# Out-projection of a hybrid decoder step: the order of VectorE's and ScalarE's work over its last six jobs

## The chip, the cores and the metric

One core of a Trainium2 chip runs the whole program. The metric is the device time of one execution in microseconds (us); lower is better. TensorE (PE) multiplies, VectorE (DVE), ScalarE (ACT) and GpSimd (POOL) work elementwise, SyncE (SP) issues the DMAs. Each engine takes its instructions strictly in the order in which they are written for it; they meet only through semaphores.

## The reference

One layer of a causal decoder over 1024 prompt tokens and 32 tokens of eight decoding sequences, width 1024, all in float32. The part that matters here:

```
mix = concat(attention(xn), short_conv(xn))      # xn = rms_norm(x)
h   = x + mix @ w_out                            # out-projection, 1024 x 1024
hn  = rms_norm(h, norm_ffn_g)                    # the second norm
y   = h + (silu(hn @ w_gate) * (hn @ w_up)) @ w_down     # FFN, hidden width 2816
out = rms_norm(y, norm_final_g)
```

with `rms_norm(x, g) = x * rsqrt(mean(x*x) + 1e-6) * g` over the 1024 channels. The program also returns the new keys, values and convolution states.

## The kernel before

Activations lie transposed: channels on the 128 partitions in KT = 8 tiles, 1056 tokens along the free axis in NC = 3 chunks of CH = 352 columns. A float32 product is made of three passes over operands split into a high and a low part (`act_hi`, `act_lo` for activations, `w_hi`, `w_lo` for weights). A *job* is one output tile n of one chunk c: 8 tiles x 3 passes = 24 matmuls of 352 columns into one of the PSUM banks 0 to 5.

The out-projection has 24 jobs in the order OUT_ORDER: c outer and n = 0, 1 inner (jobs 0 to 5), then n = 2, 3, 4 over all chunks (6 to 14), then for each chunk n = 5, 6, 7. So chunk 0 is complete with job 17, chunk 1 with job 20, chunk 2 with job 23. For every job

- VectorE adds the bank to the residual (`add_product`, line 1441; it counts `h_done`),
- ScalarE squares the new residual tile into one of six slots (`square`, line 1005; `h_sq`),
- VectorE adds the square to the chunk's running sum `ssum` (`add_squares`, lines 1448 and 1451; `h_ss`). In the kernel before this is called for job j - 1 behind the product of job j.

When a chunk's sum is complete, TensorE sums it over the partitions with a matrix of ones (`sum_of_squares`, line 805, into bank 6 or 7). Sum 0 stands behind job 18, sum 1 behind job 22 (SUMS_BEHIND = [18, 22]), and sum 2 behind the first job of the FFN:

```
pe.wait_ge(h_ss, chunk_end(c))      # 18, 21 and 24 additions
...
if i == 0:
    sum_of_squares(2)
```

Then `mean_square` (VectorE, line 1131), `take_root` (ScalarE, a Sqrt, line 886) and the reciprocal (VectorE, line 1137) give the chunk's factor. The normalised tile k of the chunk is made by `normal` (VectorE, line 1138, into one of two slots of `out32`), copied to `act_hi` by ScalarE (`normal_hi`, line 881), and its rest is put into `act_lo` by VectorE (`low`, line 1146). Eight such tiles make `norm(1, c)`. Slot i is free when the low part of i - 2 is done.

In the kernel before VectorE does the whole norm of chunk 0 behind product 18; products 19 to 22 with their additions, the mean of chunk 1, product 23 and the last two additions follow; then come norm 1, the mean of chunk 2 and norm 2. ScalarE follows the same order.

The first group of the FFN has 12 jobs, chunk outer and n inner (`FIRST_JOBS`: two gate tiles n = 0, 1 and two up tiles n = 2, 3). The first job of a chunk waits for all eight low parts of that chunk (`lo_done`). The up tiles n = 2, 3 reuse the banks of the gate tiles and wait for ScalarE's Silu of these (line 1011, `first_silu`, called one by one with `next(first_silus)`; those not yet taken are taken in `gates(0, 0, first=True)`). ScalarE loads a table when it changes between Sqrt and Silu.

GpSimd splits each weight unit of 128 x 1024 that the DMAs bring into `w_hi` (a cast, line 393) and `w_lo` (a subtraction, line 395), with a small gate instruction (line 391) ahead of them that waits until the unit three places before has been used. The first three units of the FFN follow the ends of jobs 21, 22 and 23, the fourth has a place of its own and follows directly. SyncE loads a unit as soon as the split of the unit two places before is done. POOL's and SP's orders are not touched by the diff.

Of the kernel before, what the change touches and what calls it, by code (L numbers as in the profile page):

```python
# [30 lines left out]
KT = D // P  # L31
# [4 lines left out]
NC = 3  # L36
# [33 lines left out]
def f32(ap):  # L70
    return ap.bitcast(F32)


def build(nc, xT, w, gains, taps, conv_state, state_k, state_v, yT, kT, v_out, conv_tail):
    with ExitStack() as ctx:
# [147 lines left out]
        def norm_slot(i):  # L223

            return out32[:, 2 + i % 2, :]

        def cols(c):
            return slice(CH * c, CH * (c + 1))
# [650 lines left out]
        def _(act):  # L879
            def copy(out, in_):  # L880
                return act.activation(out, in_, ACT.Copy)  # L881

            def take_root(which, c):
                act.wait_ge(mean_sq, NC * which + c + 1)
                r = rstd if which else r_in
                act.activation(r[:, cols(c)], r[:, cols(c)], ACT.Sqrt).then_inc(root, 1)

            def normal_hi(c, ks=range(KT)):
                for k in ks:
                    i = KT * c + k  # L890
                    act.wait_ge(y_done, i + 1)
                    copy(act_hi[:, k, cols(c)], norm_slot(i)).then_inc(hi_done, 1)
# [21 lines left out]
            for j in range(QK_JOBS, QK_JOBS + V_JOBS):  # L914
# [4 lines left out]
                i = j - QK_JOBS  # L919
# [80 lines left out]
            def square(which, j):  # L1000
                n, c = H_ORDERS[which][j]
                act.wait_ge(h_done, NC * KT * which + j + 1)
                if j >= 6:
                    act.wait_ge((h_ss, last_ss)[which], j - 5)
                act.activation(sq6[j % 6], res[:, n, cols(c)], ACT.Square).then_inc(h_sq, 1)

            def first_silu():

                for i, (f, c) in enumerate(FIRST_GATES):
                    act.wait_ge(job_done, OUT_JOB0 + 24 + FIRST_JOBS.index((f, c)) + 1)  # L1010
                    yield act.activation(silu[:, f, cols(c)], ps[:, 3 * f + c, 0:CH], ACT.Silu).then_inc(silu_done, 1)

            first_silus = first_silu()
            for j in range(NC * KT):
                square(0, j)
                if j in SUMS_BEHIND:
                    take_root(1, SUMS_BEHIND.index(j))
                if j == SUMS_BEHIND[0]:
                    normal_hi(0)
            next(first_silus)  # L1020
            normal_hi(1, range(0, 2))
            next(first_silus)
            normal_hi(1, range(2, 8))
            take_root(1, 2)
            normal_hi(2, range(0, 3))
            next(first_silus)
            normal_hi(2, range(3, 6))
            next(first_silus)
            normal_hi(2, range(6, 8))

            def gates(it, g, first=False):
                job = 72 * it + FFN_JOB0 + 36 * g
# [40 lines left out]
        def _(dve):  # L1073
# [50 lines left out]
            def mean_square(which, c):  # L1124

                if which == 0:
                    dve.wait_ge(ss_done, c + 1)
                else:
                    dve.wait_ge(ss_all, NC * (which - 1) + c + 1)
                bank = (c % 2, 6 + c % 2, c)[which]  # L1130
                dve.tensor_scalar((rstd if which else r_in)[:, cols(c)], ps[:, bank, 0:CH], 1.0 / D, EPS, ALU.mult, ALU.add).then_inc(mean_sq, 1)

            def normal(which, c, k, dst):

                if k == 0:
                    dve.wait_ge(root, NC * which + c + 1)
                    chain(dve.reciprocal(rstd[:, cols(c)], rstd[:, cols(c)]))  # L1137
                dve.scalar_tensor_tensor(dst, res[:, k, cols(c)], g_sb[:, which, k:k + 1], rstd[:, cols(c)],  # L1138
                                         ALU.mult, ALU.mult).then_inc(y_done, 1)

            def norm(which, c):

                def low(i):
                    k = i % KT
                    dve.wait_ge(hi_done, i + 1)
                    dve.tensor_tensor(act_lo[:, k, cols(c)], norm_slot(i), f32(act_hi[:, k, cols(c)]),  # L1146
                                      ALU.subtract).then_inc(lo_done, 1)

                for k in range(KT):
                    i = KT * c + k  # L1150
                    if i >= 2:
                        dve.wait_ge(lo_done, i - 1)
                    normal(which, c, k, norm_slot(i))
                    if k >= 1:
                        low(i - 1)
                low(KT * c + KT - 1)

            def raw_low(k):

# [274 lines left out]
            def add_product(which, j):  # L1434

                n, c = H_ORDERS[which][j]
                dve.wait_ge(job_done, (OUT_JOB0, LAST_JOB0)[which] + j + 1)
                if which == 0:
                    dve.wait_ge(x2_in[n], 16)
                bank = j % 6 if which == 0 else last_bank(j)  # L1440
                dve.tensor_tensor(res[:, n, cols(c)], ps[:, bank, 0:CH], res[:, n, cols(c)],  # L1441
                                  ALU.add).then_inc(h_done, 1)

            def add_squares(j):
                n, c = OUT_ORDER[j]
                dve.wait_ge(h_sq, j + 1)
                if n == 0:
                    dve.tensor_copy(ssum[:, cols(c)], sq6[j % 6]).then_inc(h_ss, 1)
                else:
                    dve.wait_ge(h_ss, OUT_ORDER.index((n - 1, c)) + 1)  # L1450
                    dve.tensor_tensor(ssum[:, cols(c)], ssum[:, cols(c)], sq6[j % 6], ALU.add).then_inc(h_ss, 1)

            for j in range(NC * KT):
                add_product(0, j)
                if j >= 1:
                    add_squares(j - 1)
                if j in SUMS_BEHIND:
                    mean_square(1, SUMS_BEHIND.index(j))
                if j == SUMS_BEHIND[0]:
                    norm(1, 0)  # L1460
            add_squares(NC * KT - 1)
            norm(1, 1)
            mean_square(1, 2)
            norm(1, 2)

            def hidden_of(it, g, first=False):
                for i in range(6):
# [8 lines left out]
            with dve.Fori(0, 5) as it:  # L1476
                for g in (1, 2):
                    hidden_of(it, g)
                    for i in range(NC * KT):
                        n, c = divmod(i, NC)  # L1480
# [83 lines left out]
SUMS_BEHIND = [18, 22]  # L1564
# [6 lines left out]
def last_bank(i):  # L1571

    return 3 + i % LAST_RING
# [165 lines left out]
```

## Time and profile before

| what | us |
|---|---|
| median of 3 runs | 1337.97 |
| lowest, highest | 1336.29, 1338.19 |
| the profiled execution, its own time | 1337.92 |
| its span, first to last instruction | 1336.1 |
| TensorE busy in the span | 1303.4 |
| VectorE busy | 474.6 |
| ScalarE busy | 238.3 |
| GpSimd busy | 504.9 |

The profiled execution took 1.8 us more than its span, and stands 0.05 under the median. TensorE is busy nearly throughout, so the table alone says little of any other engine: what they do matters only where TensorE waits for them. All times in the rows below are us from the start of the span.

### The profile page before, as it was taken

What the parts mean: (1) busy time and instruction counts of PE and PEld (TensorE: products, weight loads), DVE (VectorE), ACT (ScalarE), POOL (GpSimd) and SP (SyncE); (2) the same over time, 40 slices, a digit from 0 to 9 for tenths busy, and PEclk for the clock granted to TensorE, in tenths of its full rate; (3) what the DMA queues carried; (4) which work ended last, traced back from release to release, by engine and by line L of the source; (5) the groups of instructions that cost most, each with busy time, mean ns of one, the idle gap of its engine ahead of it and who ended that gap; (6) DMA issues with size and microseconds to landing.
All of it is one profiled execution on the core that took longest, in us unless ns stands there. A gap on an engine that the chain in (4) does not pass through costs nothing.

```text
span 1336.1 us, 20793 instructions
## 1 busy us (share of the span) xinstructions
PE 1303.4 (98%) x8488; PEld 1224.6 (92%) x8488; DVE 474.6 (36%) x884; ACT 238.3 (18%) x505; POOL 504.9 (38%) x476
## 2 busy tenths in 40 slices
PE   6999999999899999899999999999999999999996
PEld 6999987989565699899999999999999999999996
DVE  5854222344565432860212222221213130303056
ACT  6000110000666511331000010101010101010114
POOL 3443143222464332406434343434333333444435
PEclk9999999999999999999999999999999999999998
DMA  5534566252111131101111111111111111110103
GB/s 194 186 136 179 183 222 236 69 199 79 48 64 64 35 128 48 47 18 64 48 48 48 48 48 48 48 46 37 45 48 48 48 48 48 46 50 32 63 1 132
DMA packets 37940, 107.84 MB, mean 81 GB/s; under 512 B 4000, under 2 KB 16352, under 8 KB 36064
## 3 DMA queue, kind: packets, MB, share of 16 engines
q1 hardware_dynamic: 37856, 106.60, 22.4%
q8 instruction: 67, 1.10, 0.3%
q14 instruction: 17, 0.14, 0.0%
HBM read 95.73 MB, written 10.85 MB: 80 GB/s over the span
## 4 chain that ended last, share of the span: by engine, by line
PE 68%; DVE 4%; issue 1%; ACT 1%; DVEq 0%; ACTq 0%
PE ps L507 14%; PE ps L508 14%; PE ps L509 14%; PE ps L858 6%; PE ps L860 6%; PE ps L859 6%; PE ps L649 2%; PE ps L692 2%; PE ps L673 2%; DVE out L1138 1%; PE ps L667 1%; DVE work L1137 1%; DVE resid L1500 0%; DVE resid L1343 0%; DVE act_lo L1146 0%
## 5 line engine op out<-in xcount | busy, mean ns | idle before, releaser
L507 PE MATMUL ps<-act_hi,w_hi 128*128 128x352 f32 x1608 | 522.8, 325 | 10.5 <-DVE act_lo L1161 10.2
L508 PE MATMUL ps<-act_lo,w_hi 128*128 128x352 f32 x1608 | 516.5, 321 | 0.0
L509 PE MATMUL ps<-act_hi,w_lo 128*128 128x352 f32 x1608 | 516.3, 321 | 0.0
L507 PEld LDWEIGHTS ps<-act_hi,w_hi 128*128 128x128 f32 x1608 | 302.6, 188 | 24.6 <-issue 23.7
L508 PEld LDWEIGHTS ps<-act_lo,w_hi 128*128 128x128 f32 x1608 | 303.1, 188 | 0.2
L509 PEld LDWEIGHTS ps<-act_hi,w_lo 128*128 128x128 f32 x1608 | 302.3, 188 | 0.0
L391 POOL TENSOR_TENSOR gate_cell<-ones 128x1 f32<-128x1 f32 x92 | 18.1, 197 | 676.7 <-PE ps L509 462.0
L395 POOL TENSOR_TENSOR w_lo<-w_stage,w_hi 128x1024 fp32r<-128x1024 f32 x95 | 233.3, 2456 | 7.6
L1472 DVE TENSOR_TENSOR work<-ps,work 128x352 f32<-128x352 f32 x66 | 34.4, 524 | 443.4 <-PE ps L509 443.4
L858 PE MATMUL ps<-pair_hi,w_hi 128*128 128x352 f32 x504 | 162.7, 323 | 0.0
L1482 DVE TENSOR_TENSOR resid<-ps,resid 128x352 f32<-128x352 f32 x240 | 126.0, 525 | 102.7 <-PE ps L860 102.7
L859 PE MATMUL ps<-pair_lo,w_hi 128*128 128x352 f32 x504 | 162.2, 322 | 0.0
L860 PE MATMUL ps<-pair_hi,w_lo 128*128 128x352 f32 x504 | 162.1, 322 | 0.0
L393 POOL CAST w_hi<-w_stage 128x1024 fp32r<-128x1024 f32 x95 | 99.2, 1044 | 19.5 <-DVE work L1169 9.5
L1040 ACT ACTIVATE work<-ps 128x352 f32<-128x352 f32 x60 | 27.9, 465 | 401.3 <-PE ps L509 401.3
L860 PEld LDWEIGHTS ps<-pair_hi,w_lo 128*128 128x128 f32 x504 | 94.8, 188 | 0.0
L859 PEld LDWEIGHTS ps<-pair_lo,w_hi 128*128 128x128 f32 x504 | 94.7, 188 | 0.0
L858 PEld LDWEIGHTS ps<-pair_hi,w_hi 128*128 128x128 f32 x504 | 94.7, 188 | 0.0
L881 ACT ACTIVATE pair_hi<-work 128x352 fp32r<-128x352 f32 (+1 forms) x70 | 36.9, 531 | 289.5 <-DVE work L1472 211.1
L440 POOL TENSOR_SCALAR q_blk<-ident,row_rec 128x128 f32<-128x128 f32 x64 | 43.1, 685 | 78.3 <-DVE row_rec L1352 78.3
L471 POOL TENSOR_TENSOR pair_lo<-work,pair_hi 128x352 fp32r<-128x352 f32 x66 | 60.6, 948 | 0.0
L1441 DVE TENSOR_TENSOR resid<-ps,resid 128x352 f32<-128x352 f32 x48 | 25.0, 522 | 56.5 <-PE ps L509 47.9
(216 smaller groups left out, 1316.0 us busy)
## 6 DMA issues: line engine op xcount, KB each, us to landing
w_stage<-in_w SPq DMA_DIRECT2D x98, 512.0 KB, 3.5
resid<-in_state_k SPq DMA_DIRECT2D x8, 1792.0 KB, 8.0
v_buf<-in_state_v SPq DMA_DIRECT2D x14, 1024.0 KB, 5.2
resid<-in_xT SPq DMA_DIRECT2D x16, 528.0 KB, 7.5
out_yT<-resid SPq DMA_DIRECT2D x24, 176.0 KB, 1.8
q_d<-out SPq DMA_DIRECT2D x12, 176.0 KB, 4.3
out_kT<-out SPq DMA_DIRECT2D x12, 176.0 KB, 1.8
out_v<-out SPq DMA_DIRECT2D x16, 128.0 KB, 1.9
```

The lines of the kernel that those rows point to most:

```text
L393: pool.tensor_copy(hi, w_stage[:, stage, :]).then_inc(w_split, 1)
L395: pool.tensor_tensor(lo, w_stage[:, stage, :], f32(hi), ALU.subtract).then_inc(w_split, 1)
L440: pool.tensor_scalar(recip[t % 4][h], ident[:, :], row_rec[:, x:x + 1], None, ALU.mult).then_inc(spread, 1)
L471: pool.tensor_tensor(pair_lo[:, 2 * (g % 2) + f, cols(c)], silu[:, f, cols(c)], f32(pair_hi[:, 2 * (g % 2) + f, cols(c)]), ALU.subtract).t ...
L507: pe.matmul(out, hi, rhs_hi, start=first, stop=False)
L508: pe.matmul(out, hi, rhs_lo, start=False, stop=False)
L509: return pe.matmul(out, lo, rhs_hi, start=False, stop=last)
L858: pe.matmul(out, hi, x_hi, start=(f == 0), stop=False)
L859: pe.matmul(out, hi, x_lo, start=False, stop=False)
L860: mm = pe.matmul(out, lo, x_hi, start=False, stop=(f == 1))
L881: return act.activation(out, in_, ACT.Copy)
L1482: dve.tensor_tensor(res[:, n, cols(c)], ps[:, 6 + i % 2, 0:CH], res[:, n, cols(c)], ALU.add).then_inc(added, 1)
```

## The change

Only the order of calls in VectorE's and ScalarE's programs changes, from job 0 of the out-projection to the norm of chunk 2. Squares are added directly behind the product of the same job. The products and additions of jobs 19 to 23 are put between the tiles of the norms of chunks 0 and 1: 19 and 20 inside norm 0, 21 and 22 between the norms, 23 inside norm 1, that is behind chunk 1's reciprocal and its first two normals. `norm` becomes `normals`, which takes a range of tiles. ScalarE squares in the same places; it takes all Silus but the first two behind norm 2, where before two more stood inside it.

```diff
@@ ScalarE @@
             first_silus = first_silu()
-            for j in range(NC * KT):
+            for j in range(SUMS_BEHIND[0] + 1):
                 square(0, j)
-                if j in SUMS_BEHIND:
-                    take_root(1, SUMS_BEHIND.index(j))
-                if j == SUMS_BEHIND[0]:
-                    normal_hi(0)
+            take_root(1, 0)
+            normal_hi(0, range(0, 2))
+            square(0, 19)
+            normal_hi(0, range(2, 5))
+            square(0, 20)
+            normal_hi(0, range(5, 8))
+            square(0, 21)
+            square(0, 22)
+            take_root(1, 1)
+            normal_hi(1, range(0, 2))
+            square(0, 23)
+            normal_hi(1, range(2, 5))
             next(first_silus)
-            normal_hi(1, range(0, 2))
+            normal_hi(1, range(5, 8))
             next(first_silus)
-            normal_hi(1, range(2, 8))
             take_root(1, 2)
-            normal_hi(2, range(0, 3))
-            next(first_silus)
-            normal_hi(2, range(3, 6))
-            next(first_silus)
-            normal_hi(2, range(6, 8))
+            normal_hi(2, range(0, 8))
@@ VectorE @@
-            def norm(which, c):
+            def normals(which, c, ks):
...
-                for k in range(KT):
+                for k in ks:
                     i = KT * c + k
                     if i >= 2:
                         dve.wait_ge(lo_done, i - 1)
                     normal(which, c, k, norm_slot(i))
                     if k >= 1:
                         low(i - 1)
-                low(KT * c + KT - 1)
+                    if k == KT - 1:
+                        low(i)
...
-            for j in range(NC * KT):
+            for j in range(SUMS_BEHIND[0] + 1):
                 add_product(0, j)
-                if j >= 1:
-                    add_squares(j - 1)
-                if j in SUMS_BEHIND:
-                    mean_square(1, SUMS_BEHIND.index(j))
-                if j == SUMS_BEHIND[0]:
-                    norm(1, 0)
-            add_squares(NC * KT - 1)
-            norm(1, 1)
+                add_squares(j)
+            mean_square(1, 0)
+            normals(1, 0, range(0, 2))
+            add_product(0, 19)
+            normals(1, 0, range(2, 3))
+            add_squares(19)
+            normals(1, 0, range(3, 5))
+            add_product(0, 20)
+            normals(1, 0, range(5, 6))
+            add_squares(20)
+            normals(1, 0, range(6, 8))
+            add_product(0, 21)
+            add_squares(21)
+            add_product(0, 22)
+            mean_square(1, 1)
+            add_squares(22)
+            normals(1, 1, range(0, 2))
+            add_product(0, 23)
+            normals(1, 1, range(2, 3))
+            add_squares(23)
+            normals(1, 1, range(3, 8))
             mean_square(1, 2)
-            norm(1, 2)
+            normals(1, 2, range(0, 8))
```

## Rows read from the trace of the kernel before

**Rows 1.** The page, busy us, share of the span and instructions of each engine.
```profile
PE 1303.4 (98%) x8488; PEld 1224.6 (92%) x8488; DVE 474.6 (36%) x884; ACT 238.3 (18%) x505; POOL 504.9 (38%) x476
```

**Rows 2.** Waits of TensorE from 530 to 600: in total, times, longest.
```profile
PE ps L805 <- DVE work L1451: 3.9, 3, 2.3
```

**Rows 3.** Timeline, TensorE: start, duration, line, tiles, [idle before <-releaser].
```profile
535.42 0.32 PE L509 MATMUL ps<-act_hi,w_lo 128*128 128x352 f32 x1
536.78 0.86 PE L805 MATMUL ps<-work,ones 128*128 128x352 f32 x2 [1.05 <-DVE work L1451]
...
552.58 0.32 PE L509 MATMUL ps<-act_hi,w_lo 128*128 128x352 f32 x1
555.19 1.54 PE L805 MATMUL ps<-work,ones 128*128 128x352 f32 x2 [2.29 <-DVE work L1451]
...
564.88 0.32 PE L509 MATMUL ps<-act_hi,w_lo 128*128 128x352 f32 x1
565.72 0.86 PE L805 MATMUL ps<-work,ones 128*128 128x352 f32 x2 [0.52 <-DVE work L1451]
...
585.91 0.43 PE L507 MATMUL ps<-act_hi,w_hi 128*128 128x352 f32 x1 [0.26 <-ACT work L1011]
```

**Rows 4.** Windows: PE, PEld, DVE, ACT, POOL busy (instructions), granted clock, DMA.
```profile
557.80:558.20 0.40, 0.40 (x3) 0.40 (x2) 0.37 (x1) 0.00 (x0) 0.00 (x0) 0.50 0.00 0
```

**Rows 5.** Timeline, VectorE.
```profile
531.96 0.53 DVE L1441 TENSOR_TENSOR resid<-ps,resid 128x352 f32<-128x352 f32 x1 [2.86 <-PE ps L509]
...
535.77 0.53 DVE L1441 TENSOR_TENSOR resid<-ps,resid 128x352 f32<-128x352 f32 x1 [2.86 <-PE ps L509]
...
541.16 1.08 DVE L1138 SCALAR_TENSOR_TENSOR out<-resid,g_sb,work 128x352 f32<-128x352 f32 x2
...
548.66 1.17 DVE L1146 TENSOR_TENSOR act_lo<-out,act_hi 128x352 fp32r<-128x352 f32 x2
...
551.46 2.27 DVE L1451 TENSOR_TENSOR work<-work 128x352 f32<-128x352 f32 x1
...
554.09 1.04 DVE L1451 TENSOR_TENSOR work<-work 128x352 f32<-128x352 f32 x1
...
555.49 2.24 DVE L1451 TENSOR_TENSOR work<-work 128x352 f32<-128x352 f32 x1
...
561.38 0.53 DVE L1441 TENSOR_TENSOR resid<-ps,resid 128x352 f32<-128x352 f32 x1 [3.21 <-PE ps L509]
561.82 3.85 DVE L1451 TENSOR_TENSOR work<-work 128x352 f32<-128x352 f32 x2
565.59 2.34 DVE L1137 RECIPROCAL work<-work 128x352 f32<-128x352 f32 x1
567.96 1.97 DVE L1138 SCALAR_TENSOR_TENSOR out<-resid,g_sb,work 128x352 f32<-128x352 f32 x2
```

**Rows 6.** Timeline, GpSimd: casts (line 393) and subtractions (line 395) of the weight splits.
```profile
549.36 1.36 POOL L393 CAST w_hi<-w_stage 128x1024 fp32r<-128x1024 f32 x1
550.81 2.54 POOL L395 TENSOR_TENSOR w_lo<-w_stage,w_hi 128x1024 fp32r<-128x1024 f32 x1
...
553.73 1.03 POOL L393 CAST w_hi<-w_stage 128x1024 fp32r<-128x1024 f32 x1
554.84 2.52 POOL L395 TENSOR_TENSOR w_lo<-w_stage,w_hi 128x1024 fp32r<-128x1024 f32 x1
...
562.74 2.55 POOL L395 TENSOR_TENSOR w_lo<-w_stage,w_hi 128x1024 fp32r<-128x1024 f32 x1
...
566.64 2.40 POOL L395 TENSOR_TENSOR pt_lo<-w_stage,pt_hi 128x1024 fp32r<-128x1024 f32 x1
```

**Rows 7.** Timeline, ScalarE: table loads and a Sqrt.
```profile
536.85 1.28 ACT L886 ACT_TABLE_LOAD   x1
...
576.97 1.28 ACT L886 ACT_TABLE_LOAD   x1
578.27 0.50 ACT L886 ACTIVATE work<-work 128x352 f32<-128x352 f32 x1
```

## The prediction

> **What bounds the kernel.** The page's shares come first: TensorE is busy 98% of the span, so only time in which it waits or runs slowly can be won, and only time that it newly waits can be lost [rows 1]. The waits of TensorE in the stretch of the change come second: 3.9 us in three waits of the column sums (line 805) for VectorE's addition of squares (line 1451) [rows 2]. The timeline of TensorE shows where they are [rows 3]. For its pace, VectorE takes up the products of successive jobs 3.815 us apart (531.96, 535.77), which makes 24 matmuls 0.159 us apart [rows 5]. Between sum 0 (536.78) and the last matmul of job 22 (552.58) lie 15.80 us, four jobs (15.26) less one matmul step (0.16) and 0.70 more: a column sum itself costs 0.70, before any wait.
>
> With that pace the whole excess of the stretch can be dated [rows 3]:
> - before sum 0: 536.78 - 535.42 - 0.16 = 1.20;
> - before sum 1: 555.19 - 552.58 - 0.16 = 2.45;
> - from sum 1 to the last matmul of the first FFN job: 564.88 - 555.19 = 9.69, where a sum and two jobs less a step take 8.17, so 1.52 for the half clock. The granted clock there is 0.50 (1.2 GHz) until 558.2, after TensorE had stood still 2.3 us [rows 3, 4];
> - before sum 2: 565.72 - 564.88 - 0.16 = 0.68;
> - before the gate job of chunk 1 that waits for a Silu: sum 2, 0.70 and five jobs end at 585.50, it starts at 585.91: 0.4.
>
> Together 6.3 us, 0.47% of the span. That is all the change can win here. 0.2% (2.7 us) is about what a measurement of this kernel can tell from no change.
>
> **Why the sums wait.** Additions of squares that should take 0.52 take 2.27, 1.04 and 2.24 [rows 5]. Laid beside GpSimd's splits [rows 6] each follows one pattern: an addition issued while GpSimd works ends some 0.38 after GpSimd's instruction (553.35 to 553.73, 554.76 to 555.13, 557.36 to 557.73; the last one of squares 565.29 to 565.67). It works the other way too: a cast issued under VectorE's last low part (ends 549.83) ends 0.89 after it, at 550.72, and a subtraction behind a short addition ends 2.24 after that addition. A normal (line 1138) is held likewise: issued 567.96, the two take 1.97 instead of 1.08, behind the subtraction that ends at 569.04. A reciprocal is not (issued at 565.59, under the last cast and the subtraction at 566.64, it takes 2.34), nor are the products (line 1441), which read PSUM. The rows fit one rule: VectorE instructions with two SBUF inputs and GpSimd's split instructions exclude each other, first come first served.
>
> The Trainium skill ("SBUF — State Buffer", section "Who interferes with whom") says the same in general: a VectorE instruction with two SBUF inputs, or one in a two-port mode, and a GpSimd instruction that reads SBUF block each other for the whole instruction. It speaks against this change, and the trace agrees with it in the four additions above.
>
> What the holds are worth is worked out from rows below: without them the new order would win 5.3 us, with them it loses 2.6.
>
> **What is removed.** Adding squares at once takes add_squares(17) from behind product 18 to some 1.1 us behind product 17, near 533. Sum 0 then starts when job 18 ends, at 535.58: 1.20 gained. Jobs 19 to 22 follow 1.20 earlier; results reach VectorE at 540.3, 544.1, 547.9 and 551.7. For chunk 0's root little changes: the mean is earlier, but ScalarE's table load starts after the square at 536.85 and takes 1.28, so the Sqrt (0.50) starts at 538.15 [rows 7]. The reciprocal (2.35) ends at 541.04, 0.1 earlier than before.
>
> **VectorE in the new order.** Before, norm 0 was eight normals and eight low parts at 1.06 a pair, 541.16 to 549.83 [rows 5]. I lay the new list out with product 0.45 to the next start, addition 0.52, pair 1.06. Normals 0 and 1 and low 0 end at 542.75, product 19 is issued 542.67, its addition ends 544.58; product 20 is issued 546.50, its square (ScalarE, as long as the Sqrt) ends 547.56, and add_squares(20) ends at 548.4. Sum 1 needs only that and job 22 (551.54): its wait of 2.45 and the half clock behind it, 1.52, go. So far 5.2 us are gained. The cover is 3.1 us.
>
> Now GpSimd. Its three gated splits follow jobs 21, 22 and 23 (job ends 547.7, 551.5, 556.1), with a fourth behind them, so 548.5 to 565 is nearly all cast and subtraction. With the rule:
> - cast until 549.80; low 5 ends 550.19; subtraction until 552.43, which holds normal 7 until 552.82; low 6 553.26; cast until 554.15, low 7 554.54. Norm 0 ends 1.5 before the first FFN job needs it (556.06): no wait, but 4.7 later than before.
> - product 21 554.99, square 21 ends 555.52, but add_squares(21) is held by a subtraction until 557.17 (before: done 557.73 under the same holds). Product 22 557.6, mean 1, add_squares(22) 558.73.
> - ScalarE's Sqrt for chunk 1 ends 558.60; reciprocal until 561.00. It now stands ahead of product 23, with normals 8 and 9 and low 8. Cast until 562.51; low 8 is held by the last subtraction (562.59 to 565.14) until 565.53.
> - product 23 ends 565.98, its result having waited since 556.4; normal 10, low 9; add_squares(23) ends 567.36.
>
> Sum 2 needs add_squares(23). TensorE has finished the first FFN job at 559.88, so it stands 7.5 us and starts sum 2 at 567.40, 1.7 later than before (565.72). The 5.2 gained are given back here, and 1.7 more: product 23 and its addition took 4.3 us before, from 561.38 on, and now take 11 from the time the result is there. Queued behind the waiting sum are all later FFN jobs.
>
> **Clock.** A stop of 7.5 us is longer than the one of 2.3 that cost 1.52. How much a longer one costs no row shows. The cost lies after the return of TensorE; 0.5 if the clock rises soon after, 3.0 (twice the measured) if it stays low twice as long. I take the measured 1.5.
>
> **Behind sum 2.** Five jobs, 0.70 and 1.5 put the gate job that needs the third Silu at 567.40 + 0.70 + 19.08 + 1.5 = 588.7. ScalarE now issues this Silu behind the whole of norm 2: low 15 ends 573.96 (five more normals and lows, undisturbed, after a small wait for a Silu), table load and Sqrt 575.82, reciprocal 578.21, eight pairs: last normal 585.84, copy 586.37, table load 1.28, Silu 588.16. It is just hidden (0.5), and it is a floor: with a cheaper clock the job would still not start before 588.2. Before it started at 585.91 and lost 0.1 more at its first matmul. So the sum is 588.7 - 585.9 - 0.1 = 2.7 late by TensorE, 2.2 by ScalarE's floor; I take 2.6. From there on the same jobs at the same pace, GpSimd's next split only after gate tiles of the FFN, no weight later than its job (the last split ends 565.1, its first job is at 577): the delay passes to the end whole. Weights' DMAs are issued in the same order, no other queue is touched.
>
> On the page "ScalarE: Activation LUTs", section "What ACT_TABLE_LOAD costs", the Trainium skill adds a drain of about 1.38 us to each load. Here a Sqrt follows 0.02 behind the end of its load (576.97 + 1.28, 578.27) [rows 7], so the trace has no such drain; by the page the floor would be 2.8 later and the time 1342.9. Its chance is nil by these rows.
>
> The profiled execution took 1337.92 for a span of 1336.1 and agrees with the median, 1337.97. 1337.97 + 2.6 = 1340.6.
>
> **Rivals.**
> - *Forecast* (0.45), 1340.6, own range 1339.5 to 1341.8. Half of it lies beyond 0.2%.
> - *It breaks even* (0.20). For: the order in which GpSimd and VectorE get their turn is guessed where both are queued; one hold fewer (the 2.2 of low 8, if VectorE runs normals 8, 9 and low 8 in one go) puts add_squares(23) near 565.2, the chain behind it 2.2 earlier: 1338.4. Against: other turn orders that I laid out only move the hold and end within 0.6 of 567.4.
> - *Slower by more* (0.23). The clock stays low twice as long (3.0) and the first FFN job waits for a low 7 held once more (0.8): 567.8 + 0.7 + 19.1 + 3.0 = 590.6, so 4.6 late: 1342.6.
> - *Faster* (0.12), the other side: the holds cost little in the new order, because VectorE's instructions fall between GpSimd's. Undisturbed, the same list ends add_squares(23) at 559.96; sum 2 starts at 560.0, the Silu then bounds the gate job at 580.6, 5.3 earlier: 1332.7. Against it: thirteen two-input instructions stand between 548.4 and the end of add_squares(23), and from 548.5 to 565.1 GpSimd pauses only for moments between its instructions. It decides if add_squares(23) ends before 563.
>
> **Chances.** Faster by over 0.2%: 0.12 (of the last). Within: 0.42 (0.22 forecast, 0.20 break-even). Slower: 0.46 (0.23 forecast, 0.23 above). The range 1337.3 to 1343.0 leaves out the faster case and the ends of the clock's cost.
>
> **What would show it.** Right: no wait of sums 0 and 1, granted clock 1.00 through 551 to 560, one wait of TensorE for line 1451 of about 7.5 us near 560 to 567 with the clock at half behind it, low 8 and add_squares(21) much longer than 0.52, product 23 issued near 565. Wrong: sum 2 starting before 563; a wait of the first FFN job for norm 0; a Silu wait above 1 us at the gate job, which would add to the delay.

## The result, and the profile after

| what | before | after |
|---|---|---|
| median, us (6 runs each) | 1337.13 | 1342.02 |
| lowest, highest | 1336.29, 1338.19 | 1341.27, 1342.18 |
| the profiled execution, its own time | 1337.92 | 1342.18 |
| its span | 1336.1 | 1340.4 |

The ratio is 1.0032, 95% interval 1.0022 to 1.0042: slower by 4.9 us between the medians, which alone give 1.0037. The forecast was 1340.6, 2.6 more than a median of 1337.97; the median of its first three runs stood above that of six. 1342.02 lies inside the stated range (1337.3 to 1343.0) and 0.2 above the forecast's own range (1339.5 to 1341.8).

In the kernel after, lines have moved: a product of VectorE is line 1445, an addition of squares 1455, the mean 1134, the reciprocal 1140, a normal 1141, a low part 1149. The sum (805), the splits (391 to 395) and the Silus (1011) kept theirs. All of the profile after stands later from the program's first part on, 0.85 at 40 us and 0.81 from 340: product 0 of the out-projection starts at 471.88, in the profile before at 471.07. No order was changed ahead of it. So 0.81 is to be taken off every time below before it is compared with the rows of before.

Waits of TensorE from 530 to 620, kernel after:

```profile
PE ps L805 <- DVE work L1455: 7.5, 1, 7.5
```

Three waits of 3.9 together [rows 2] have become one of 7.5. TensorE's timeline says which sum it is:

```profile
536.38 0.75 PE L805 MATMUL ps<-work,ones 128*128 128x352 f32 x2
...
552.23 0.75 PE L805 MATMUL ps<-work,ones 128*128 128x352 f32 x2
...
560.29 0.32 PE L509 MATMUL ps<-act_hi,w_lo 128*128 128x352 f32 x1
568.14 1.54 PE L805 MATMUL ps<-work,ones 128*128 128x352 f32 x2 [7.53 <-DVE work L1455]
```

Sums 0 and 1 follow their jobs with no wait. TensorE could start sum 2 at 560.45 (the last matmul and one step) and starts it at 568.14, which is 567.33 with the offset taken off. The granted clock in windows of half a microsecond (PE busy, matmuls, clock, DMA):

```profile
564.00:564.50 0.50, 0.00 (x0) 0.96 0.97 385
564.50:565.00 0.50, 0.00 (x0) 0.50 0.23 90
...
570.50:571.00 0.50, 0.50 (x4) 0.50 0.07 16
571.00:571.50 0.50, 0.50 (x4) 0.72 0.00 0
571.50:572.00 0.50, 0.50 (x5) 1.00 0.00 0
```

It falls from 2.4 to 1.2 GHz while TensorE stands still and is back some 3.1 us after TensorE has returned. VectorE from product 21 to addition 23:

```profile
554.33 0.51 DVE L1445 TENSOR_TENSOR resid<-ps,resid 128x352 f32<-128x352 f32 x1
555.41 2.76 DVE L1455 TENSOR_TENSOR work<-work 128x352 f32<-128x352 f32 x1 [0.57 <-ACT work L1005]
...
562.05 3.80 DVE L1141 SCALAR_TENSOR_TENSOR out<-resid,g_sb,work 128x352 f32<-128x352 f32 x2
...
566.21 0.51 DVE L1445 TENSOR_TENSOR resid<-ps,resid 128x352 f32<-128x352 f32 x1
...
567.57 0.51 DVE L1455 TENSOR_TENSOR work<-work 128x352 f32<-128x352 f32 x1
```

and GpSimd's splits beside it:

```profile
549.13 1.84 POOL L393 CAST w_hi<-w_stage 128x1024 fp32r<-128x1024 f32 x1
...
555.38 2.40 POOL L395 TENSOR_TENSOR w_lo<-w_stage,w_hi 128x1024 fp32r<-128x1024 f32 x1
...
561.86 1.03 POOL L393 CAST pt_hi<-w_stage 128x1024 fp32r<-128x1024 f32 x1
562.97 2.50 POOL L395 TENSOR_TENSOR pt_lo<-w_stage,pt_hi 128x1024 fp32r<-128x1024 f32 x1
```

Addition 21 ends at 558.17, 0.39 after the subtraction that ran from 555.38 to 557.78. The two normals in front of product 23 take 3.80 where they took 1.08 undisturbed [rows 5]: the first ends behind the cast (562.89), the second 0.38 behind the last subtraction (565.47). Product 23, an instruction that nothing holds, stands behind them and takes 0.51 from 566.21 on.

ScalarE's third Silu, with its table load:

```profile
587.28 1.28 ACT L1011 ACT_TABLE_LOAD   x1
588.57 0.46 ACT L1011 ACTIVATE work<-ps 128x352 f32<-128x352 f32 x1
```

It is in time: the job that needs it has no wait in the list of waits. The Silu starts 0.01 behind the end of its table load, and the load 0.02 behind the copy ahead of it. So here too there is no drain of about 1.38 us at a change of tables, such as the Trainium skill states ("ScalarE: Activation LUTs", section "What ACT_TABLE_LOAD costs").

### The profile page after: what moved, and what is told of

Read it like the earlier page. It is cut to its first block, busy times and chain, and to the rows that moved or that the text cites. A ratio compares the mean times of both kernels' runs of the same rounds, so it can differ in the third digit from the quotient of the medians.

```text
span 1340.4 us, 20793 instructions
## 1 busy us (share of the span) xinstructions
PE 1303.1 (97%) x8488; PEld 1225.1 (91%) x8488; DVE 472.7 (35%) x884; ACT 238.8 (18%) x505; POOL 506.3 (38%) x476
## 4 chain that ended last, share of the span: by engine, by line
PE 69%; DVE 3%; issue 2%; ACT 1%; DVEq 0%; ACTq 0%
PE ps L507 14%; PE ps L508 14%; PE ps L509 14%; PE ps L858 6%; PE ps L859 6%; PE ps L860 6%; PE ps L649 2%; PE ps L692 2%; PE ps L673 2%; PE ps L667 1%; DVE out L1141 0%; DVE resid L1347 0%; DVE work L1140 0%; DVE act_lo L1149 0%; DVE resid L1517 0%
## 5 line engine op out<-in xcount | busy, mean ns | idle before, releaser
L1499 DVE TENSOR_TENSOR resid<-ps,resid 128x352 f32<-128x352 f32 x240 | 126.1, 525 | 102.7 <-PE ps L860 102.7
L962 ACT ACTIVATE resid<-resid,row_neg 128x384 f32<-128x384 f32 (+5 forms) x48 | 42.1, 881 | 1.1 <-DVE row_neg L1347 0.6
```

The lines of the kernel that those rows point to most:

```text
L962: act.activation(prow(t, h), prow(t, h), ACT.Exp, scale=-1.0, bias=row_neg[:, x:x + 1], accum_out=row_sum[:, x:x + 1]).then_inc(exped, 1)
L1499: dve.tensor_tensor(res[:, n, cols(c)], ps[:, 6 + i % 2, 0:CH], res[:, n, cols(c)], ALU.add).then_inc(added, 1)
```

## The measure used for the experiments

Executions differ by up to 1.9 us in when the out-projection begins (product 0 between 470.76 and 472.64 in fourteen profiles), so the traces are compared by one stretch: from the start of product 0 of the out-projection to the start of VectorE's last product of the first FFN group. It holds all that the change touches. "Half clock" is the time between 550 and 598 that the granted clock was 0.50, summed over windows of half a microsecond.

| kernel | stretch, us | half clock, us | median (runs) | ratio to before, 95% |
|---|---|---|---|---|
| before | 138.03 | 3.4 | 1337.13 (6) | |
| b1, before again | 138.28 | 3.4 | 1338.31 (1) | |
| b2, before again | 136.71 | 0 | 1336.32 (1) | |
| after | 141.07 | 6.8 | 1342.02 (6) | 1.0032 (1.0022 to 1.0042) |
| a1, after again | 140.76 | 6.8 | 1340.88 (1) | |
| a2, after again | 142.09 | 10.2 | 1341.57 (8) | 1.0028 (1.0018 to 1.0039) |
| e1 | 134.69 | 0 | 1335.07 (11) | 0.9985 (0.9976 to 0.9994) |
| e2 | 132.63 | 0 | 1332.83 (7) | 0.9971 (0.9959 to 0.9982) |
| e3 | 140.75 | 3.4 | 1341.09 (7) | 1.0028 (1.0017 to 1.0040) |
| e4 | 134.01 | 0 | 1333.95 (10) | 0.9972 (0.9962 to 0.9981) |
| e5 | 140.85 | 6.8 | 1341.40 (6) | 1.0030 (1.0017 to 1.0042) |
| e6 | 141.51 | 6.8 | 1341.45 (6) | 1.0030 (1.0018 to 1.0043) |
| e7 | 139.96 | 6.8 | 1340.74 (9) | 1.0025 (1.0015 to 1.0035) |
| e8 | 132.01 | 0 | 1331.85 (5) | 0.9960 (0.9947 to 0.9974) |

The kernel before was timed beside them: 1337.72 (24 runs) beside e1 to e4, 1337.12 (15) beside e5 to e8, 1338.84 (one) beside b1, b2 and a1, 1337.94 (12) beside a2.

## Experiments on the holds

A *hold* is the time that a VectorE instruction with two SBUF inputs stands until GpSimd's cast or subtraction is done.

**e1, the kernel after without the splits' work.** The splits of the first three FFN units work on one column instead of 1024 (the other 1023 are left out, so the FFN's result is wrong), and the fourth waits until the last addition is done.

```diff
+                n = 1 if short else 1024
-                pool.tensor_copy(hi, w_stage[:, stage, :]).then_inc(w_split, 1)
+                pool.tensor_copy(hi[:, 0:n], w_stage[:, stage, 0:n]).then_inc(w_split, 1)
...
+                    if u == FFN0 + 3:
+                        pool.wait_ge(h_ss, 24)
...
+                      short=(FFN0 <= u < FFN0 + 3))
```

> The changed kernel with GpSimd's splits of the first three FFN weight units cut to one column (the other 1023 columns of these units keep what the slots held, so the FFN result is wrong) and the fourth unit's split put behind add_squares(23). GpSimd then holds nobody while VectorE works at norm 0 and jobs 19 to 23. If the holds are what delays add_squares(23) (my theory): sum 2 waits under 0.5 us, the clock stays at 1.00, the Silu behind norm 2 bounds the gate job, and the time is 3 to 4 us under the kernel before, 1333.5. If the new order is too long by itself, with or without holds (rival): sum 2 still waits 4 us or more and the time stays at 1339 or above. If the holds only matter in part: between the two.

**e2, the same in the kernel before.** The order of VectorE and ScalarE is that of before, the edit that of e1.

> The kernel before with the same cut (FFN result wrong in the same way). Sum 0 still waits 1.2 us, because add_squares(17) stands behind product 18. My theory: sums 1 and 2 do not wait and the clock does not fall, 5 us under the kernel before, 1332. Rival (sum 1 waits because all of norm 0 stands ahead of product 19 and the additions, holds or none): sum 1 still waits over 1.5 us and the gain stays under 3 us.

In e1 sum 2 starts when the first FFN job ends. The sum, then VectorE's product 23, its addition and a held low part:

```profile
559.74 0.86 PE L809 MATMUL ps<-work,ones 128*128 128x352 f32 x2
```
```profile
557.81 0.52 DVE L1449 TENSOR_TENSOR resid<-ps,resid 128x352 f32<-128x352 f32 x1
...
559.17 0.52 DVE L1459 TENSOR_TENSOR work<-work 128x352 f32<-128x352 f32 x1
...
561.82 2.73 DVE L1153 TENSOR_TENSOR act_lo<-out,act_hi 128x352 fp32r<-128x352 f32 x1
```

Product 23 starts 7.4 us earlier than after, counted from product 0 (86.90 against 94.33), and its addition takes 0.52. Only where the fourth split runs, from 559.75 on, are a normal (1.24) and a low part (2.73) still held. So in this order the holds are what makes TensorE stand 7.5 us; without them it does not stand. The Trainium skill ("SBUF — State Buffer", section "Who interferes with whom") says that a VectorE instruction with two SBUF inputs contends with a GpSimd instruction that reads SBUF. This case agrees, and e1 adds the size: the wait of 7.5 and the half clock behind it go, and of the stretch 6.4 us.

Against the kernel before e1 wins 3.3 of the stretch, where the prediction had 5.3 for this order undisturbed. It is not quite undisturbed: the two holds of the fourth split take 2.9 more than the two instructions alone, inside norm 1, and the job that needs the third Silu starts 111.50 behind product 0, 2.0 later than the prediction's 580.6 (109.53 behind it).

The third Silu, called late:

```profile
582.41 0.43 PE L511 MATMUL ps<-act_hi,w_hi 128*128 128x352 f32 x1 [2.31 <-ACT work L1015]
```

e2 is 2.2 us faster than e1 by the medians and 2.1 by the stretch. Its one wait is 1.0 at sum 0. At the start of sum 2 e1 is 1.05 ahead (88.83 behind product 0, e2 89.88), and behind it loses 3.1, of which 2.3 are the wait for the Silu. So with these holds gone the new order is still no gain over that of before; its late Silus cost more than its early sums win.

## Experiments on the order

**e3, product 23 ahead of norm 1.** From the kernel after:

```diff
@@ ScalarE @@
-            normal_hi(1, range(0, 2))
             square(0, 23)
-            normal_hi(1, range(2, 5))
+            normal_hi(1, range(0, 5))
@@ VectorE @@
             add_squares(22)
-            normals(1, 1, range(0, 2))
             add_product(0, 23)
-            normals(1, 1, range(2, 3))
             add_squares(23)
-            normals(1, 1, range(3, 8))
+            normals(1, 1, range(0, 8))
```

> The changed kernel with product 23 and add_squares(23) ahead of chunk 1's reciprocal and first normals (square 23 ahead of the copies too), Silus where the change has them. My theory: sum 2 waits under 0.5 us, but the wait comes back two jobs later: Silu 0 stands behind five copies of norm 1, so the first up tile waits some 6.5 us for it with the half clock behind, and the time is that of the changed kernel within 1 us, 1341.5. Rival (the position of product 23 is the whole loss): no such wait, 1333 to 1334.

**e4, e3 and the Silus where they were before.** As e3, and ScalarE takes the Silus one by one around and within the norms of chunks 1 and 2, as before (ScalarE's part, without the lines that it takes out):

```diff
             square(0, 23)
             next(first_silus)
+            normal_hi(1, range(0, 2))
             next(first_silus)
+            normal_hi(1, range(2, 8))
             take_root(1, 2)
+            normal_hi(2, range(0, 3))
+            next(first_silus)
+            normal_hi(2, range(3, 6))
+            next(first_silus)
+            normal_hi(2, range(6, 8))
```

> As the kernel with product 23 ahead, and the Silus back where the kernel before has them: the first ahead of chunk 1's copies, the second behind two of them, the third and fourth inside norm 2. My theory: waits of TensorE under 1 us each (for low 15 at the first job of chunk 1, for the third Silu), clock 1.00 throughout, 4.5 to 5 us under the kernel before, 1332.5. Rival (holds by GpSimd delay norm 1 so much that the first job of chunk 1 waits instead): a wait of over 3 us there and at most 2 us won.

**e5, only the last two Silus put back.** The last five lines of that diff alone. VectorE and the first two Silus are as in the kernel after.

> The changed kernel with only the third and fourth Silu put back inside norm 2. My theory: these are just hidden in the changed kernel (Silu 2 ends at about the time at which its gate job is ready, because sum 2 is late already), so nothing changes: 1342.0, within 0.7 us of the changed kernel, and sum 2 still waits 7.5 us. Rival (the Silus behind norm 2 are a cost beside that of sum 2): 2 us or more faster than the changed kernel, 1340 or below.

**e6, e3 with the first two Silus early and the other two late.** ScalarE as in e4 up to `take_root(1, 2)`, then `normal_hi(2, range(0, 8))` whole.

> The kernel with product 23 and the Silus as before (1333.95), with the third and fourth Silu moved behind norm 2 as in the change. My theory: with sum 2 no longer late, this place costs: the gate job waits 5 to 6 us for Silu 2 with the half clock behind, some 5 us slower than that kernel, 1339 to 1340. Rival (Silus behind norm 2 are harmless): 1334.

Waits of TensorE in e3:

```profile
PE ps L507 <- ACT work L1011: 5.2, 1, 5.2
PE ps L805 <- DVE work L1454: 1.7, 1, 1.7
```

Two positions of VectorE's list take the wait at sum 2 from 7.5 to 1.7. But e3 is no faster than the kernel after (1.0028 against 1.0032): sum 2 starts 5.8 us earlier (90.47 behind product 0, after 96.26), and the first Silu still stands behind norm 1's fifth tile, so TensorE stops there instead, 5.2 us, and the clock falls there. ScalarE in e3:

```profile
569.54 0.50 ACT L881 ACTIVATE act_hi<-out 128x352 fp32r<-128x352 f32 x1 [0.56 <-DVE out L1140]
570.05 1.28 ACT L1011 ACT_TABLE_LOAD   x1
571.35 0.46 ACT L1011 ACTIVATE work<-ps 128x352 f32<-128x352 f32 x1
```

With the Silus early as well (e4) only the 1.7 is left, the clock stays at 2.4 GHz, and the stretch is 134.01: 7.1 us less than after and 4.0 less than before. e5 has product 23 late and the last two Silus back:

```profile
568.91 1.54 PE L805 MATMUL ps<-work,ones 128*128 128x352 f32 x2 [7.53 <-DVE work L1459]
```

It waits 7.53 where the kernel after does, and the time is the same within the intervals. So while sum 2 is late the last two Silus cost nothing, and with sum 2 early (e3) the first one costs what was won: the late parts cover for each other. All four Silus put back with product 23 still late was not run; in the kernel after the first two have no wait of TensorE either.

e6 waits for the third Silu. The first matmul of that job, and the windows of 2 us behind it (PE busy, matmuls, clock, DMA):

```profile
587.12 0.66 PE L507 MATMUL ps<-act_hi,w_hi 128*128 128x352 f32 x1 [5.50 <-ACT work L1011]
```
```profile
588.00:590.00 2.00, 2.00 (x9) 0.50 0.00 0
590.00:592.00 2.00, 2.00 (x9) 0.50 0.00 0
592.00:594.00 2.00, 2.00 (x14) 1.00 0.00 0
```

It came out slower than expected (1341.45 against 1339 to 1340). A floor set by ScalarE, as the prediction worked it out, is there, and TensorE then works 4.9 us at half clock, which costs 2.4, not 1.5.

**e7, the first line of the change alone.** The kernel before with every addition directly behind its own product, norm 0 whole as before.

```diff
                 add_product(0, j)
-                if j >= 1:
-                    add_squares(j - 1)
+                add_squares(j)
...
-            add_squares(NC * KT - 1)
```

> The kernel before with one part of the change alone: add_squares(j) directly behind add_product(j) for all 24 jobs; norm 0 stays whole behind product 18. My theory: sum 0 no longer waits (1.2 us won), sum 1 still waits 2 to 3 us with the half clock behind, sums and Silus else as before: 1 to 1.5 us faster than the kernel before. Rival (waiting for ScalarE's square before each addition costs VectorE more than it gives): no faster, or slower.

This was the worst of my expectations: 3.6 us slower by the medians, 1.9 by the stretch. Sum 0 does start 1.20 earlier, but sum 1 now waits 6.2:

```profile
558.60 1.54 PE L805 MATMUL ps<-work,ones 128*128 128x352 f32 x2 [6.23 <-DVE work L1451]
```

VectorE ahead of it:

```profile
548.84 1.42 DVE L1138 SCALAR_TENSOR_TENSOR out<-resid,g_sb,work 128x352 f32<-128x352 f32 x1
550.18 3.15 DVE L1146 TENSOR_TENSOR act_lo<-out,act_hi 128x352 fp32r<-128x352 f32 x2
...
554.32 2.70 DVE L1451 TENSOR_TENSOR work<-work 128x352 f32<-128x352 f32 x1 [0.56 <-ACT work L1005]
556.95 0.51 DVE L1441 TENSOR_TENSOR resid<-ps,resid 128x352 f32<-128x352 f32 x1
558.02 0.53 DVE L1451 TENSOR_TENSOR work<-work 128x352 f32<-128x352 f32 x1 [0.56 <-ACT work L1005]
```

The gate of the first split follows a job of TensorE, so the first cast comes 1.3 earlier too, counted from product 0, while norm 0 on VectorE begins within 0.1 of when it began (it hangs on ScalarE's table load [rows 7]). Now the last tiles of norm 0 meet the first split, and norm 0 ends 2.7 later than before. Sum 1 also needs additions 19 and 20, each of which waits 0.56 for its own square. Sum 1 starts 2.6 later than before: about the 2.7 by which norm 0 is late. No run separates this from the two waits of 0.56, so that the moved collision is the cause is read from the trace and not tested by itself.

**e8, all of it, with sum 2 later.** The kernel before with products 19 to 23 between the tiles of both norms, additions 22 and 23 behind tiles 5 and 6 of norm 1, and sum 2 three FFN jobs later, so that TensorE need not stand for it. The second FFN job waits for product 21 in its place. The Silus come early. (In the cut below TensorE's part is whole; VectorE's is without the lines that it takes out.)

```diff
@@ TensorE @@
+                        if i == 1:
+                            pe.wait_ge(h_done, 22)
                         tile_job(3 * (n % 2) + c, c, None if n == 3 else (FFN0 + n) % RING)
-                        if i == 0:
+                        if i == 3:
                             sum_of_squares(2)
@@ VectorE, from product 21 on @@
+            add_product(0, 21)
+            normals(1, 0, range(7, 8))
+            add_product(0, 22)
+            mean_square(1, 1)
+            add_squares(21)
+            normals(1, 1, range(0, 1))
+            add_product(0, 23)
+            normals(1, 1, range(1, 6))
+            add_squares(22)
+            normals(1, 1, range(6, 7))
+            add_squares(23)
```

> A version that is to beat both: products 19 to 23 between the tiles of both norms, additions 22 and 23 behind tiles 5 and 6 of norm 1, sum 2 behind the fourth FFN job instead of the first, with a wait of the second FFN job for product 21 (its bank), and Silus early. By the rule of the holds no wait of TensorE over 0.5 us is left from job 18 to the end of the first FFN group, clock 1.00: 6 us under the kernel before, 1 to 1.5 us under the kernel with product 23 and the Silus, about 1332.3. Rival (with sum 2 so late norm 2 is): the first job of chunk 2 or its Silu waits over 1 us and the time is not below 1333.5.

No wait of TensorE is listed from 530 to 620, and sum 2 follows its job at the usual step:

```profile
570.93 0.32 PE L509 MATMUL ps<-act_hi,pt_lo 128*128 128x352 f32 x1
571.09 0.75 PE L805 MATMUL ps<-work,ones 128*128 128x352 f32 x2
```

VectorE is held as before, but nothing that TensorE needs at once stands behind it:

```profile
562.30 2.59 DVE L1148 SCALAR_TENSOR_TENSOR out<-resid,g_sb,work 128x352 f32<-128x352 f32 x1
...
568.42 0.52 DVE L1462 TENSOR_TENSOR work<-work 128x352 f32<-128x352 f32 x1
```

The stretch is 6.0 us shorter than before, of the 6.3 of excess that the prediction dated. e8 beats both kernels: 1331.85, ratio 0.9960 (0.9947 to 0.9974).

## Experiments on the size

By the two first traces the change costs 3.0 us of the stretch, by the medians 4.9. Both kernels were run again to see what differs between executions of the same program.

> The kernel before, unchanged, looked at once more. Open is where the rest of the measured loss comes from: the medians stand 4.9 apart, the two profiled stretches from job 18 to the end of the first FFN group 3.0. If executions of the kernel before differ in whether the clock falls behind the 2.3 us wait of sum 1, this one shows either a granted clock of 1.00 behind that wait and 1.5 us less between job 18 and the end of the group, or the same 1.5 again. If the rest lies ahead of the stretch (arrival of the first loads), the time of product 0 (471.1 in the profile before) differs.

> The same once more; two more looks say whether the cost of the clock (0 or 1.5 us), the step of the matmuls behind it and the time of product 0 vary from execution to execution.

> The changed kernel, unchanged, looked at once more. Theory: sum 2 again waits 7.5 us, and the clock again costs about 1.5 us behind it; between 0.5 and 3.0 if it depends on the moment of the return. The matmuls of the 40 us behind it again start 0.161 us apart instead of 0.159 if that belongs to the long stop, 0.159 if it was of that execution alone.

> The changed kernel once more, now timed in rounds beside the kernel before. Theory: the kernel before has two kinds of execution, those in which the clock falls behind the 2.3 us stop at sum 1 (mean granted clock up to 0.995, about 1338.1) and those in which it doesn't (0.996 and above, about 1336.8), so its executions lie in two groups some 1.3 apart; the changed kernel always falls behind its stop of 7.5 us (all executions at 0.995 or below) and is 2.6 to 3.9 slower than the first group, 4 to 5 slower than the second: median near 1341.5, ratio 1.0025 to 1.0035. Rival: the difference between 2.6 (by the trace) and 4.9 (by the medians) is a cost of the new order outside this stretch; then the profile shows more than 141.2 us from product 0 to the last product of the first FFN group, or more than 0.5 added behind it.

b1 repeats the profile before (half clock 3.4, stretch 138.28). b2 has the same three waits as the profile before (3.9 together, 2.3 the longest) and sum 1 stands the same 2.3 us. But the clock does not fall:

```profile
552.00:554.00 2.00, 0.77 (x5) 1.00 0.00 0
554.00:556.00 2.00, 0.98 (x4) 1.00 0.73 250
556.00:558.00 2.00, 2.00 (x15) 1.00 0.07 20
```

In the profile before it was at 0.50 at 557.8 [rows 4]. The 1.52 of the half clock is missing from b2's stretch, which is 1.3 to 1.6 shorter than that of before and b1. So the kernel before has two kinds of execution. The mean granted clock that comes with each time sorts them: of its 51 timed executions beside e1 to e8 and a2, 28 have 0.996 or more, with a median of 1336.8, and 23 have 0.995 or less, with 1338.2. (Three of the 28 lie at 1338.0 to 1338.4, so the mean clock is not a perfect mark.) e1, whose one wait is 2.3 too, sorts in the same way: six executions of 0.996 or more with a median of 1334.4, five of 0.995 or less with 1336.1. e2's five of 0.996 or more have 1332.8, so e2 stays faster than e1 when like is compared with like, by some 1.6. All 14 executions of the kernel after, a2's among them, have 0.994 or less, and in its three profiles the clock falls in the stop of 7.5 us each time.

a1 waits 7.5 at sum 2 as well, and its stretch is 140.76: 2.73 more than before, 2.48 more than b1, 4.05 more than b2. In a2 the clock falls earlier in the stop and comes back later:

```profile
562.00:564.00 2.00, 0.00 (x0) 0.59 0.72 246
564.00:566.00 2.00, 0.00 (x0) 0.50 0.22 45
566.00:568.00 2.00, 0.87 (x3) 0.50 0.60 221
568.00:570.00 2.00, 2.00 (x8) 0.50 0.01 4
570.00:572.00 2.00, 2.00 (x9) 0.50 0.00 0
572.00:574.00 2.00, 2.00 (x12) 0.85 0.00 0
```

TensorE returned at 567.13 and had the full clock again at about 572.6: 5.5 us at half, 2.7 lost, where the profile after lost 1.5 (3.1 at half) and a1 1.7 (3.5 at half). The rival of a2 named 141.2 as its mark, and 142.09 is above it; yet most of the excess over a1 (1.33) lies in this half clock, inside the stretch, and the rest in a slower step of the matmuls (last section). Behind the stretch nothing was added: from its end to the last sum over channels (line 796) it is 718.86 in a2 and 718.83 in before and a1.

One thing ahead of the stretch does differ. e5 and e7 are the two profiles with a mean granted clock of 0.991, and both have one more spell of half clock, 6.8 us long, near 340 to 348, in a part that no edit touches. In e5:

```profile
344.00:346.00 2.00, 2.00 (x10) 0.50 0.00 0
```

VectorE's instructions, laid beside those of the profile before, are later behind it than ahead of it by 1.40 in e5 and by 1.37 in e7. None of the 51 executions of the kernel before has a mean clock of 0.991, nor has any of a2's eight. Of the first six executions of the kernel after three have it, and 1342.01 and 1342.03, between which its median lies, are two of them. No such execution of the kernel after was traced, so whether they had this spell is not shown.

## Why the prediction was right, and where its size was off

Step by step, with 0.81 taken off the times of the profile after:

- **Sums 0 and 1 stop waiting, 5.2 gained.** Right against the profile before. Against the executions that b2 shows, only 3.65 of it was there to gain, since 1.52 was a clock that had not fallen. That is one term that was mis-sized.
- **The holds.** Right. Addition 21 was put at a done time of 557.17 and ended at 557.36; product 23 was put at 565.98 and ended at 565.91; addition 23 at 567.36, and it ended at 567.27. In detail it was normal 9 and not low 8 that the last subtraction held; the sum is the same, as the prediction said of other turn orders. Normal 7 was held by the cast and not by the subtraction behind it, and norm 0 ended at 553.60, 0.9 before the forecast 554.54.
- **Sum 2 waits 7.5 and starts at 567.40.** It waited 7.5 and started at 567.33, 1.61 later than before.
- **The clock costs 1.5 again.** 1.48 in the profile after, 1.65 in a1, 2.7 in a2. The bound of 3.0 was needed: it is not a rival apart but something that happens in some executions of this same mechanism. The other half of that rival (*slower by more*), a first FFN job that waits for low 7, is in no profile.
- **The third Silu is just hidden.** Right: no wait, and the Silu ended at 588.22, where the floor was put at 588.16. e6 shows such a floor as a real one, as soon as sum 2 is early: there the job starts at 587.12 and has waited 5.5.
- **The delay passes whole to the end.** Right: 718.83 behind the stretch in before and in a1. The profile after has 0.40 more there.
- **Agreement with the median.** This was where 1340.6 came from: 2.6 was put on 1337.97, the median of three, and the median of six is 0.84 lower. By the medians the cost is 4.9 and not 2.6, 2.3 more, so a part of why 1340.6 came within 1.4 of 1342.02 is luck: the base was too high by 0.84. Against executions in which the clock had fallen, the change cost 2.5 to 2.7 by a1, as forecast; against the others 4.05. A median over both kinds lies 3.6 (a2's batch) to 4.9 (the first six) below the kernel after.

The own times of the two profiled executions stand 4.26 apart: 0.81 ahead of product 0, 3.04 in the stretch and 0.40 behind it. The 0.81 is of that execution (a1 has 0.23, and a2 begins 0.18 earlier than the profile before). The 3.04 are 1.61 at sum 2, 1.48 for the clock, 0.53 back because the Silu is in time, and 0.48 from a slower step of the matmuls, 0.161 instead of 0.159 us from 571 to 613. a1 has not that step, so it does not come with the change as such. What else the 4.9 of the medians holds is in part that the median of before lies among executions without the fall. How much of the remainder a longer half clock carries (a2), how much the spell near 340 that e5 and e7 have, and how much is chance in six runs, is not settled. So what failed in size is twofold: the 5.2 to be gained, 3.65 in about half of the executions, and the half clock at 1.5, up to 2.7.

The rival "it breaks even" rested on one hold fewer, and none was missing. "Faster" had its condition (addition 23 done before 563) in e1, e3, e4 and e6; of these only e1 and e4 were faster than before, by 0.15% and 0.28%; e1 has most of its splits left out. e3 and e6 show that the condition was not enough: the Silus had to come early too.

## What to carry to other kernels

Before work of one engine is moved, write down which of its instructions a neighbour holds and what stands behind them for the bounding engine; here moving a product behind two held instructions cost more than all the waits that the change removed. Where two late things stand one behind the other on the path (sum 2 and the Silus), undoing one may show nothing; e3, e5 and e4 had to be read together. A time won on the bounding engine also moves everything that is gated by it (e7's splits came 1.3 earlier), and a sum that nobody needs soon is better put later on the bounding engine (e8) than hurried on the engine that feeds it.

## What was not expected of the hardware

- The same stop of 2.3 us dropped the clock to 1.2 GHz in two profiles (before, b1) and not in a third (b2); the 7.5 us stop dropped it in every one. What it costs is about half the time between TensorE's return and the rise, which was 3.0 us in the profile before, 3.1 after, 3.5 in a1, 4.9 in e6 and 5.5 in a2.
- A longer stop does not always mean a longer half clock: it was 3.4 us at e3's stop of 5.2, 6.8 at e6's of 5.5, and 6.8 (after, a1) or 10.2 (a2) at the same stop of 7.5.
- The clock can fall where nothing was changed and other executions keep it: near 340 in e5 and e7, at a cost of 1.4 us.
- A cast of GpSimd issued while VectorE runs one two-input instruction behind the other takes longer: 1.84 at 549.13 in the profile after, where the one at 561.86 took 1.03. It ended 0.9 behind low 5, the last of them before VectorE had to wait.
- A matmul step of 0.161 us in place of 0.159 for some 40 us appears in some profiles (after, a2, e3, e4, e6, e7), for some 20 us in e1, and not in others (before, a1, b1, b2, e2, e5, e8). Its cause is open; a long stop is not enough (a1) and not needed (e4).
